# Hybrid pooling and S5 block on one core: partial sums of the paired products kept in PSUM, and two more pairs

## What is computed

```python
h = rmsnorm(x, norm_pre) * (1 + scale) + shift
u_pool, z_pool, u_ssm, z_ssm, g_pool, g_ssm = split(h @ w_in)      # each 1024 x 1024
y_pool = causal_pool_mixer(u_pool, pool_w, pool_scale) * silu(z_pool)
y_ssm = s5_mixer(u_ssm, ...) * silu(z_ssm)                          # a state-space layer
merged = sigmoid(g_pool) * (y_pool @ w_branch_pool) + sigmoid(g_ssm) * (y_ssm @ w_branch_ssm)
out = x + gate * rmsnorm(merged @ w_out, norm_post)
```

## Time and profile before

| | us |
|---|---|
| median of 3 runs | 962.59 |
| lowest, highest | 962.35, 963.3 |
| the profiled execution | 962.82 |
| its span, first to last instruction | 961.0 |
| granted clock of PE, mean | 0.998 of full |

### The profile page before, as it was taken

The page is one execution under the profiler, slowest core; times in us unless marked ns, Lnnn a source line. Parts: engine busy times, 40 slices in busy tenths (PEclk is TensorE's granted clock), DMA queues, the critical chain, the costliest instruction groups (busy, mean ns, idle before and its releaser), DMA issues.

```text
span 961.0 us, 11597 instructions
## 1 busy us (share of the span) xinstructions
PE 938.4 (98%) x4444; PEld 788.1 (82%) x4444; DVE 651.4 (68%) x906; ACT 349.0 (36%) x405; POOL 45.4 (5%) x82
## 2 busy tenths in 40 slices
PE   3999999999999999999999999999999999999997
PEld 3888878888888888888888888888888888888886
DVE  5988989988888868866787767664344434455233
ACT  5741442233333334544454554531122231223111
POOL 0019700000000000000000000000000000000000
PEclk9999999999999999999999999999999999999999
DMA  9843363445555379657567545896543359322222
GB/s 347 297 154 127 126 213 132 154 153 174 195 192 190 107 218 291 175 175 223 159 200 201 154 136 152 262 340 220 175 158 109 106 198 222 149 88 88 88 88 88
DMA packets 96871, 168.80 MB, mean 176 GB/s; under 512 B 38704, under 2 KB 55216, under 8 KB 96816
## 3 DMA queue, kind: packets, MB, share of 16 engines
q1 hardware_dynamic: 87456, 163.60, 52.0%
q10 hardware_dynamic: 9360, 4.46, 2.2%
HBM read 118.73 MB, written 49.29 MB: 175 GB/s over the span
## 4 chain that ended last, share of the span: by engine, by line
PE 92%; DVE 2%; DMA 2%; ACT 1%; SPq 1%; issue 0%; ACTq 0%; DVEq 0%
PE ps L1873 52%; PE ps L1980 17%; PE ps L2075 9%; PE psb L1980 5%; PE ps L2027 2%; PE psa L2002 1%; PE psa L1949 1%; PE psa L1873 1%; PE psb L2016 1%; PE psb L2014 1%; DMA sin_t<-yp_d 1%; DMA x_tok<-in_x 1%; PE psb L1949 0%; PE psb L1899 0%; SPq L714 0%
## 5 line engine op out<-in xcount | busy, mean ns | idle before, releaser
L1873 PE MATMUL ps<-bop,w_hi 128*128 128x512 f32 x1312 | 351.9, 390 | 1.0 <-DVE bop L1375 0.8
L1873 PEld LDWEIGHTS ps<-bop,w_hi 128*128 128x128 f32 x1312 | 245.3, 188 | 51.8 <-issue 1.0
L1873 PE MATMUL ps<-bop,w_lo 128*128 128x512 f32 x656 | 201.9, 389 | 0.0
L1873 PEld LDWEIGHTS ps<-bop,w_lo 128*128 128x128 f32 x656 | 123.1, 188 | 25.5
L1327 DVE TENSOR_TENSOR w_lo<-raw,w_hi 128x1024 fp32r<-128x1024 f32 x49 | 60.6, 1237 | 61.1 <-ACT w_hi L995 61.0
L995 ACT ACTIVATE w_hi<-raw 128x1024 fp32r<-128x1024 f32 x49 | 51.7, 1057 | 93.2 <-PE ps L1873 75.8
L1980 PE MATMUL ps<-bop,r_hi 128*128 128x512 f32 x208 | 64.1, 390 | 0.0
L1980 PE MATMUL ps<-t_hi,r_hi 128*128 128x512 f32 x140 | 55.3, 395 | 0.3 <-issue 0.3
L1980 PE MATMUL ps<-t_hi,r_lo 128*128 128x512 f32 x140 | 54.6, 390 | 0.0
L1980 PE MATMUL ps<-t_lo,r_hi 128*128 128x512 f32 x140 | 54.5, 389 | 0.0
L2075 PE MATMUL ps<-wo_hi,y_hi 128*128 128x512 f32 x128 | 49.8, 389 | 0.0
(11 more groups left out here) (313 smaller groups left out, 1537.8 us busy)
## 6 DMA issues: line engine op xcount, KB each, us to landing
raw<-in_wstream SPq DMA_DIRECT2D x58, 512.0 KB, 5.4
pair_raw<-in_wstream SPq DMA_DIRECT2D x20, 512.0 KB, 4.7
ada<-in_w_ada SPq DMA_DIRECT2D x16, 512.0 KB, 11.2
x_tok<-in_x SPq DMA_DIRECT2D x8, 512.0 KB, 6.7
gs_d<-gt SPq DMA_DIRECT2D x8, 512.0 KB, 4.2
win_d<-win_new SPq DMA_DIRECT2D x8, 512.0 KB, 4.0
wout_d<-wout_new SPq DMA_DIRECT2D x8, 512.0 KB, 5.7
wout<-wout_d SPq DMA_DIRECT2D x8, 512.0 KB, 4.3
```

What stands on the lines that cost most here:

```text
L1873: last = mm(ps[slot(u)][:, f * HALF:f * HALF + HALF], a[:, k, :], b(k, f), start=k == 0 and q == 0, stop=k == KT - 1 and q == 2)
```

## The change

- Of a pair's seven additions, four are left to PSUM. P6 is added by matmuls with start=False onto P1's bank, P7 onto that, P4 onto that; P3 onto P5's bank. ACT copies the sums between (copy_p1, copy_u2, copy_p5) and takes c21 out, with the activation function in the same step; DVE keeps c11, c12 and c22. A half product that adds waits for the copy before it.
- The order of PE becomes P1, P2, part_a, P4 and P3 of the pair before, P6, P5, P7. The last pair's P4 and P3 are run inside up(0), whose K tiles are taken in the order 4 to 7, 0 to 3.
- Two more pairs make zp(0) to zp(3). The pooling stage has only five other products between, FILL: zs(7) at m = 0, zp(4), zp(5), zp(6) at m = 2, 4, 6 and zp(7) at m = 7; m = 1, 3, 5 have none.
- yp_out writes in place of silu(z), in eight buffers of their own (zp_t); yp_d with its stores and loads is gone.
- Tables 1 and 2 are made in the pairs (CHUNKS), only table 3 in the pooling stage. SP issues the chunks' stores before load_pair.
- At m = 7, pool_low comes before rotate_in, and swap_z, rotate_out and part_c(7) move behind in_high(1), in_low(7) and bp(0).

The diff, cut to its core:

```diff
+PAIRS += [("zp", 0), ("zp", 2)]
+FILL = {0: [("zs", 7)], 2: [("zp", 4)], 4: [("zp", 5)], 6: [("zp", 6)], 7: [("zp", 7)]}
...
+        def bank_of(j, i):
+            if i in (P5, P3):
+                return (ps[0] if j % 2 else ps[1])[:, HALF * (j % 2):HALF * (j % 2) + HALF]
+            if i == P2 and j:
+                return ps[1][:, HALF:D]
+            return ps[0][:, 0:HALF] if j % 2 or i == P2 else psb[:, HALF:D]
...
@@ SP: made, loop over the pairs @@
-                    sp.wait_ge(k_ready, b + 1)
                     if b + 1 < KT:
                         load_cf(b + 1)
+                    sp.wait_ge(k_ready, b + 1)
...
             for j in range(NP):
+                if (j - 1, "b") in CHUNK_AT:
+                    made(CHUNK_AT[j - 1, "b"])
+                if (j, "a") in CHUNK_AT:
+                    made(CHUNK_AT[j, "a"])
                 if j + 2 < NP:
                     load_pair(j + 2)
...
@@ ACT: loop over the pairs @@
             for j in range(NP):
-                copy_p1(j)
                 if j:
-                    pair_high(j, P4)
-                    pair_high(j, P7)
+                    pair_high(j, P5)
+                    pair_high(j, P3)
+                    func_c22(j - 1)
                 if more:
                     pair_high(j + 1, P1)
+                copy_p1(j)
+                if more:
                     pair_high(j + 1, P2)
                 prep_out(CHUNK_AT.get((j - 1, "b")))
+                if j:
+                    c21(j - 1)
+                    pair_high(j, P7)
+                    pair_high(j, P4)
+                    func_c11_c12(j - 1)
...
+                copy_u2(j)
...
+                copy_p5(j)
                 if more:
                     pair_high(j + 1, P6)
...
@@ ACT: pooling stage @@
                 pool_high(m)
-                swap_z(m)
+                if m < KT - 1:
+                    swap_z(m)
...
-                evac(("zp", m), gt[m % 2][:, :], ACT.Silu)
-                split_hi(p + 3)
+                for u in FILL.get(m, ()):
...
+                    evac(u, dst, ACT.Silu)
+                    if u != ("zp", 7):
+                        split_hi(USE[u] + 2)
...
+            for n in range(6):
                 in_high(n)
+                if n == 1:
+                    swap_z(KT - 1)
             split_hi(USE["bp", 1])
+            for n in range(6, KT):
+                in_high(n)
+            split_hi(USE["bp", 2])
             y_out(KT - 1)
...
@@ DVE: loop over the pairs @@
                 if j:
-                    c12(j - 1)
-                    sum3(j)
-                    pair_low(j, P4)
-                    pair_low(j, P7)
+                    c22(j - 1)
+                    pair_low(j, P5)
+                    pair_low(j, P3)
                 if more:
                     pair_low(j + 1, P1)
                 prepare(CHUNK_AT.get((j, "a")))
-                u2(j)
                 c11(j)
                 if more:
                     pair_low(j + 1, P2)
+                if j:
+                    sum3(j)
+                    pair_low(j, P7)
+                    c12(j - 1)
+                    pair_low(j, P4)
+                first_tap(CHUNK_AT.get((j, "a")))
+                prepare(CHUNK_AT.get((j, "b")))
+                if more:
                     sum1(j + 1)
                     sum2(j + 1)
                     sum4(j + 1)
                     pair_low(j + 1, P6)
...
@@ DVE: pooling stage @@
-                stt(rt[n % 2][:, :], ps[slot(("pp", n))][:, :], pscale[:, n:n + 1], gt[n % 2][:, :],
+                stt(zp_t[n], ps[slot(("pp", n))][:, :], pscale[:, n:n + 1], zp_t[n],
...
-                split_lo(p + 2)
+                split_lo(USE["up", m] + 2)
+                if m == KT - 1:
+                    pool_low(m)
                 rotate_in(m)
-                pool_low(m)
+                if m < KT - 1:
+                    pool_low(m)
...
+                if m < KT - 1:
+                    rotate_out(m)
...
+            for n in range(2):
                 in_low(n)
+            yp_out(6)
+            in_low(2)
             yp_out(7)
             for n in range(3, KT):
                 in_low(n)
+            rotate_out(KT - 1)
...
@@ PE: half_product @@
                 if i == P1:
+                    if j == 1:
+                        pe.wait_ge(c11_done, 1)
+                    elif j:
+                        pe.wait_ge(c21_done, j - 1)
...
+                elif i == P6:
+                    pe.wait_ge(p1_copied, j + 1)
...
+                elif i == P7:
+                    pe.wait_ge(u2_copied, j + 1)
+                elif i == P4:
+                    pe.wait_ge(c22_done, j + 1)
                 else:
-                    pe.wait_ge(added, 7 * j + ADDS[i])
...
+                    pe.wait_ge(p5_copied, j + 1)
+                bank = bank_of(j, i)
+                adds = i in (P6, P7, P4, P3)
...
-                        last = mm(bank, a, b, start=k == 0 and q == 0, stop=k == 3 and q == 2)
+                        last = mm(bank, a, b, start=k == 0 and q == 0 and not adds, stop=k == 3 and q == 2,
+                                  skip_group_check=adds)
...
@@ PE: loop over the pairs, up(0), end of the pooling stage @@
                 part_a(CHUNK_AT.get((j - 1, "b")))
+                if j:
+                    half_product(j - 1, P4)
+                    half_product(j - 1, P3)
+                part_a(CHUNK_AT.get((j, "a")))
                 half_product(j, P6)
                 half_product(j, P5)
                 half_product(j, P7)
...
+            turn0, order0 = ("up", 0), (4, 5, 6, 7, 0, 1, 2, 3)
+            begin(turn0)
...
+            half_product(NP - 1, P4)
+            half_product(NP - 1, P3)
...
-                product(("zp", m), h)
-            product(("zs", 7), h)
+                for u in FILL.get(m, ()):
+                    product(u, h)
             pool_pair_ready(3)
             pool_product(6)
-            part_c(7)
             pool_product(7)
 
             for n in range(KT):
                 product(("bp", n), h, 0 if n == 0 else None)
+                if n == 0:
+                    part_c(KT - 1)
```

More of the change, by code:

```diff
@@ L88 @@
 SPLIT = {u: s for s, u in enumerate([u for u in USES if u[0] != "ga"])}
-FROM_TILE = 6
 P1, P2, P6, P5, P3, P4, P7 = range(7)
-S_ORDER = [(j, i) for j in range(NP) for i in (P1, P2, P6, P5, P7, P4, P3)]
+S_ORDER = []
+for j in range(NP):
+    S_ORDER += [(j, P1), (j, P2)] + ([(j - 1, P4), (j - 1, P3)] if j else []) + [(j, P6), (j, P5), (j, P7)]
+S_ORDER += [(NP - 1, P4), (NP - 1, P3)]
 S_POS = {u: n for n, u in enumerate(S_ORDER)}
-RING, BANKS = 8, 5
-ADDS = {P6: 1, P2: 2, P7: 3, P5: 5, P4: 6, P3: 7}
+W_ORDER = [(0, i) for i in range(7)]
+for j in range(NP):
+    now, then = [(j, P5), (j, P3)] if j else [], [(j, P7), (j, P4)] if j else []
+    W_ORDER += now + ([(j + 1, P1), (j + 1, P2)] if j + 1 < NP else []) + then + ([(j + 1, P6)] if j + 1 < NP else [])
+W_POS = {u: n for n, u in enumerate(W_ORDER)}
+RING = 8
 CHUNKS = [("cos", 0), ("sin", 0)]
@@ L877, in _ @@
                         load_u(m + 1)
[L878 to L883 removed]
+                load_w(USE["up", m] + 4)
+                if m == 0:
+                    made(("cos", LAST_TABLE))
+                    made(("sin", LAST_TABLE))
+                if m == 1:
+                    sp.wait_ge(job_out[slot(("zs", 7))], evicted(("zs", 7)))
+                    sp.dma_start(zs_d[7], zs_last).then_inc(zs_stored, 16)
                 if m + 2 < KT:
@@ L1211, in _ @@
             for m in range(KT):
[L1212 removed]
+                i = m // 2
                 if m:
@@ L1865, in plain, with k_step @@
                 return tuple(lambda k, f, x=x: x[:, k, f * HALF:f * HALF + HALF] for x in (hi, lo))
-            def k_step(u, k, x_hi, x_lo):
+            def k_step(u, k, x_hi, x_lo, order=range(KT)):
                 p = USE[u]
@@ L1873, in k_step @@
                         last = mm(ps[slot(u)][:, f * HALF:f * HALF + HALF], a[:, k, :], b(k, f),
-                                  start=k == 0 and q == 0, stop=k == KT - 1 and q == 2)
+                                  start=k == order[0] and q == 0, stop=k == order[-1] and q == 2)
                 return last
@@ L1991, in _ @@
                 half_product(j, P7)
-                part_a(CHUNK_AT.get((j, "a")))
-                half_product(j, P4)
-                half_product(j, P3)
+            turn0, order0 = ("up", 0), (4, 5, 6, 7, 0, 1, 2, 3)
+            begin(turn0)
+            pe.wait_ge(c21_done, NP - 1)
+            pe.wait_ge(c12_done, NP - 1)
+            for k in order0[:2]:
+                k_step(turn0, k, *h, order0)
+            half_product(NP - 1, P4)
+            half_product(NP - 1, P3)
+            for k in order0[2:]:
+                if k == 0:
+                    pe.wait_ge(b12_lo, 1)
+                last = k_step(turn0, k, *h, order0)
+            last.then_inc(mm_done, 1)
             def part_b(m):
@@ L2035, in pool_pair_ready @@
```

(7 more changed lines are left out.)

311 lines of the change are left out of this document (141 added, 170 removed).

## The result

The changed kernel takes 973.58 us (median of 4 runs, 972.94 to 974.17) against 962.72 for the kernel before in the same session: ratio 1.0112, 95% interval 1.0095 to 1.0130. Forecast were 964.8, and 961.3 to 968.3. The profiled execution took 972.94 with a span of 971.2, that is 10.2 more than before; the forecast had 2.2 more. So the direction was right, and some 8 us were missed; the time lies above the range and above the 973 of rival D.

A forecast was written before the change was run, and what follows sets the result against it. PE (TensorE) was taken as the bound, a sum of matmuls at fixed pace. -5.3 + 4.1 + 0.5 + 2.9 = +2.2 us on a 961.0 us span gave 963.2, a time of 964.8 us; range 961.3 to 968.3.

The forecast's parts named there:

- rival D: Pairs: load_pair behind k_d makes the weights late in each of eight pairs, copy_p1 past 12.8; 967 to 973 us; chance 0.12.
- The sum of matmuls: Pairs and pooling stage: two more pairs replace four zp products, PSUM additions cost PE nothing; -5.3 us.
- P6 of pair 0: First pair: P6 adds into P1's bank, so PE waits for copy_p1(0); +4.1 us, bounds 0 and 4.2.
- The later pairs: Pairs after the first: taken at nothing, 0 to 1 us for all together.
- 12 and 6 us of margin: Later pairs: 12 us before the next P6 on DVE's string; copy_p1 would have to come 6 us later to delay PE.
- The pool product: Pooling stage, m = 5: pp5 waits for evac(up6), which stands behind store_y's DMA issues; +0.5 us, 0 to 4.
- 2.7 to 5 us of margin: Pooling stage, m below 6: margin of each rotate_out before its part_c; 1.5 us at m = 6.
- The end of the pooling stage: At m = 7: bp0 waits 1.8 us for yp_out(6), part_c(7) 1.2 for rotate_out(7); together +2.9 us.
- checkpoint of 478.3 us: Stretch from the first pair to the end of the last pp product: 476.1 us before, 478.3 after.
- A's waits: The forecast case: three waits, at P6(0), a pool product and the pooling stage's end; 963.7 to 966.5 us; chance 0.50.

The follow-up runs named there:

- both edits: Changed kernel with the k_d stores moved behind load_pair on SP and copy_p1(0) put ahead of pair_high(0, P7) on ACT: 961.86 us, ratio to before 0.9987.

## Why the prediction was wrong

**The sum of matmuls** stands: with both edits the pairs take 259.33, waits of 0.6 among them, against 226.29 + 38.40 - 5.44 = 259.25 by the earlier trace rows. So -5.3 was right, and the additions in PSUM cost PE nothing here.

**P6 of pair 0**: right in place, releaser and size: P6 starts 10.11 us into the pairs, 4.11 later than the 6.00 of before (the row's 4.51 counts from the end of P2). Missed is what comes behind such a wait, 1.3 us of matmuls at 1.2 GHz. My bounds, 0 to 4.2, held only the idle time. The kernel before had a hint of it, at the one long wait of the earlier trace rows; its PE timeline, which I hadn't looked at there, has eight matmuls in 2.07 us right behind the 15.18 of idleness, and eight in 1.06 later. It is no more than a hint, since the table of stretches gives the granted clock of these first two microseconds as 1.00:

```profile
15.18 2.07 PE L1899 MATMUL psb<-diag,x_tok 128*128 128x128 f32 x8 [15.18 <-DVE diag L1354]
...
20.28 1.06 PE L1899 MATMUL psb<-diag,x_tok 128*128 128x128 f32 x8
```

**The later pairs**, the step that failed. It said "I take at nothing" and "0 to 1 us for all pairs together", and they cost 5.8, the 7.1 missed in the pairs less the 1.3 of slow matmuls at pair 0. Taken from the first matmul of pair 1 to up(0) it is 6.0: 250.74 us, against 244.75 with both edits. The rows were at hand: k_d 5.10 and the landing 4.7 in the earlier trace rows. What was wrong is the way they were used. I followed the load of pair j + 2 through one lap, from a start that I set at 14.5 us into the pair, and found 12 and 6 us of margin. But that start is itself the end of the lap before: k_ready waits for out_weights, which waits for the low part of the very weights that the load brings. A chain that closes on itself has no margin, only a length, and it was 21.7 in the lap shown and 22.0 in the mean, against 21.06. I also took the landing at its length of before (4.7), where it is 5.6 behind the stores. Rival D had the cause ("because load_pair comes behind k_d") and the sign to look for (waits that recur every 21 us), at a chance of 0.12. Its condition was wrong: it had copy_p1 late, and copy_u2 was; and "the DMA engines are half busy", which I held against it, says nothing on a ring of latencies.

**The pool product**: 0.5 forecast at pp5, behind store_y and evac(up6); 0.64 measured, but at pp4, which starts at 555.46 when DVE has ended the low part of channel 5:

```profile
553.28 2.07 DVE L1735 TENSOR_TENSOR pool_lo<-pb,pool_hi 128x1024 fp32r<-128x1024 f32 x1
```

pp5 doesn't wait. The size is a coincidence, and my "2.7 to 5 us of margin" looked at rotate_out and not at this.

**The end of the pooling stage**: 2.9 forecast, 2.5 measured (1.55 and 0.95), by the chain that I had laid out, for both waits. The drain that the Trainium skill, "ScalarE: Activation LUTs", What ACT_TABLE_LOAD costs, counts with each switch of tables would have added 1.4 us there; the trace after shows none at this place either, with the ACTIVATE 1.30 us behind the load's start, and the end came no later than the rows' sum.

```profile
604.66 1.28 ACT L1073 ACT_TABLE_LOAD   x1 [5.39 <-PE ps L1915]
605.96 1.03 ACT L1073 ACTIVATE pu<-ps 128x1024 f32<-128x1024 f32 x1
```

My checkpoint of 478.3 us "to the end of the last pp" was set wrong in the text: the 2.9 us and part_c(7) lie behind that edge. Measured was 479.5 to it. To the start of bp1, where both kernels have done the same, it is 487.0 before, 489.2 by the forecast and 497.0 after.

**The range** failed because I added up cases as if only one of them could come: A's waits and D's ring hold together. 2.2 + 5.8 (the ring) + 1.3 (the clock) + 0.7 (the pooling stage, of which 0.1 is the larger wait and 0.6 I can't place) is 10.0 of the 10.2 us.

## What to carry to other kernels

A transfer that is issued late can start a ring: load, split, compute, store, next load. Add it up all the way round and compare it with the pace of the engine that should set it; a margin found in one lap says nothing, and the loss shows only some laps later. Put what nobody waits for (here the k stores) behind what somebody does, on the queue as well as on the engine that waits for its landing. And count a long idle time of TensorE dearer than its length: the 4.5 us here cost 1.3 to 2.5 more, while waits up to 1.43 us brought no low clock.

## What the runs showed of the hardware that I had not expected

- After 4.5 us of idle PE the granted clock was 0.51 or 0.52 for 3.0 to 5.2 us. In the kernel with doubled stores, with a wait of 1.9 to 4.5 us of PE in every pair, eight such slow stretches came, of 7 to 13 matmuls; three began with the first matmul after a wait, and five 1.0 to 1.6 us behind it, when PE was already back at full pitch. One of these: a wait of 3.88, the first matmul at full pitch, the fall 1.5 us behind it.

```profile
340.35 0.47 PE L2038 MATMUL psb<-t_hi,r_hi 128*128 128x512 f32 x1 [3.88 <-ACT gt L1131]
...
341.83 0.63 PE L2038 MATMUL psb<-t_hi,r_hi 128*128 128x512 f32 x1
```

  In the changed kernel, with waits up to 1.43 us at P7, there is none in the later pairs. So the pitch of the first matmul doesn't tell whether a wait costs clock.
- The second of a pair's two stores of 512 KB, issued right behind a load of 1 MB and the first store, landed 7.3 us after its issue (changed kernel), and 9.4 where the store of win_d, another 512 KB, stood there too (kernel before with the new order on SP). It was 4.1 with both stores ahead of the load, and 3.7 behind it with eight small stores, 5 us, between (medians over the pairs of u).
- Seventeen matmuls more, in a wait, made the kernel 1.8 us faster (medians of four runs each, whose ranges don't meet).
